# Modulation sums of a two-stream transformer block: sixteen-partition pieces through HBM instead of eight transposes

## The chip, the cores and the metric

The kernel runs on one core of one Trainium2 chip. Its time is the device time of one execution in microseconds (us); lower is better. The engines are TensorE (PE), VectorE (DVE), ScalarE (ACT), GpSimd (POOL) and SyncE (SP), which only issues DMAs. Each engine works through its own instructions in order and waits on semaphores for the others.

## What is computed

Two layers (`DEPTH = 2`) work on two streams of 256 tokens of width 1024: the latents `h` and the context `hc`. Each layer has a feed-forward part, a token mixer and a second feed-forward part. All three are modulated by nine vectors that come from a conditioning vector and a big matrix:

```
mods   = split((silu(c)     @ w_ada[l] + b_ada[l]), 9)      # for h
mods_c = split( silu(c_ctx) @ w_ada[l] + b_ada[l],  9)      # for hc
h = post_norm(h, 0.5 * mods[2] * swiglu(h * (1 + mods[1]) + mods[0], ffn1_up[l], ffn1_down[l]), ln_g[l, 0], ln_b[l, 0])
...                                                          # mixer with mods[3:6], second feed-forward with mods[6:9]
swiglu(u, w_up, w_down) = (silu(u @ w_up[:, :2816]) * (u @ w_up[:, 2816:])) @ w_down
```

The modulation is the subject here: for each layer a product of two rows (c and c_ctx) with a matrix of 1024 x 9216 in float32.

## The kernel before

**Chunks.** All big products run on TensorE in chunks. A chunk of an up loop multiplies 128 columns of a weight (8 tiles of 128x128) with all 512 tokens. Each float32 weight is split into a high and a low part, and each tile takes three matmuls (L909 high times high, L910 and L911 the mixed ones), so a chunk is 24 matmuls of 128x512. The weight of a chunk is loaded by SyncE's queue into one of two raw slots (L713), ScalarE makes the high part `w_hi` (L1342), VectorE the low part `w_lo` (L1932), into one of four split slots. A chunk's split can start when the chunk four places ahead of it has been used; the load of a chunk waits for the split of the chunk two before it. A body of an up loop has four chunks (q = 0 to 3), `UP_BODIES = 11` bodies; a body of a down loop has eight chunks of 6, 6, 5 and 5 tiles, twice, in four bodies.

**Modulation blocks.** The product with `w_ada` is cut into 36 blocks of 512 columns. The first four are made at the start on TensorE. The other 32 are made beside the feed-forward loops: nine in each of three up loops (layer 0 up0 and up1, layer 1 up0), three in layer 0's down0 and two in layer 1's down0 (`ADA_OF`, `ADA_UP`, `ADA_DOWN`). Per block SyncE loads four pieces of 512 KB (L718, j = 0 to 3, two slots), and VectorE multiplies and adds them (`ada_products`, L2307 and L2310): for each of the eight row tiles and both streams one instruction of 128x512, sixteen per block, into two accumulators of 128x512. Piece j + 2 can be loaded once the products of piece j are done. The products of a block fill one body: j = 0 behind the split of q = 0, j = 1 at q = 1, and j = 2 and j = 3 one after the other at q = 2, ahead of the split of q = 3.

What is left is the sum over the 128 partitions. In the next body, behind its first chunk (q = 0), TensorE transposes both accumulators in eight pieces of 128x128 (`ada_columns`, L896) into two PSUM banks; ScalarE then sums each piece along its row with eight activations that accumulate (`ada_totals`, L1524), and VectorE adds the bias at the body's end (`ada_add`, L1971). In a down loop the transposes stand behind q = 6. The first products of the next block wait until the transposes have read the accumulators.

**What sets the order.** The order on each engine is written out by hand in the program, and semaphores tie the engines together: `lo_done` counts VectorE's splits, `ada_mul` its products (16 per block), `ada_turned` the transposed blocks, `ada_ev` the finished ones. SyncE's queue issues in program order: in each step q the weight load of a chunk of the next body, then a modulation load. GpSimd has nearly nothing to do: two clears, a few sums of the layer norm, and 44 products in the last up loop.

## Time and profile before

| | |
|---|---|
| median of 3 runs | 2436.19 us |
| lowest and highest | 2435.21, 2436.35 us |
| span of the profiled execution, first to last instruction | 2432.3 us |
| TensorE busy | 2394.7 us |
| VectorE busy | 1551.8 us |
| ScalarE busy | 1052.7 us |
| GpSimd busy | 61.6 us |
| moved by DMA | 321.83 MB, mean 132 GB/s |

The profile is of one execution. The profiled execution's own device time isn't listed beside its span; the median lies 3.9 us above the span. Times inside it are microseconds from the span's start, durations of one instruction nanoseconds where they stand in a group. A row of a timeline has the start, the duration, the engine, the line of the program, the operation and what it writes and reads; in brackets stands the idle time ahead of it and what ended that. TensorE's matmuls are pipelined, so a matmul's duration (0.39) is longer than the distance to the next start.

### The profile page before, as it was taken

What the parts mean: (1) busy time and instruction counts of PE and PEld (TensorE: products, weight loads), DVE (VectorE), ACT (ScalarE), POOL (GpSimd) and SP (SyncE); (2) the same over time, 40 slices, a digit from 0 to 9 for tenths busy, and PEclk for the clock granted to TensorE, in tenths of its full rate; (3) what the DMA queues carried; (4) which work ended last, traced back from release to release, by engine and by line L of the source; (5) the groups of instructions that cost most, each with busy time, mean ns of one, the idle gap of its engine ahead of it and who ended that gap; (6) DMA issues with size and microseconds to landing.
All of it is one profiled execution on the core that took longest, in us unless ns stands there. A gap on an engine that the chain in (4) does not pass through costs nothing.

```text
span 2432.3 us, 36421 instructions
## 1 busy us (share of the span) xinstructions
PE 2394.7 (98%) x13306; PEld 2064.5 (85%) x13306; DVE 1551.8 (64%) x2584; ACT 1052.7 (43%) x2114; POOL 61.6 (3%) x72
## 2 busy tenths in 40 slices
PE   7999999999999999999999999999999999999998
PEld 4888889887888778898888898888898888999998
DVE  6777467445545445568775367876566556667875
ACT  6533324444333434364343254343245443555544
POOL 0000000000000000020000000000000000001220
PEclk9999999999999999999999999999999999999999
DMA  8666354332222322326663326564434333556654
GB/s 277 182 186 186 97 176 119 86 87 78 61 68 71 91 84 61 113 79 200 185 187 99 96 83 206 178 187 137 143 100 121 105 96 97 163 139 182 191 159 135
DMA packets 519960, 321.83 MB, mean 132 GB/s; under 512 B 14054, under 2 KB 481552, under 8 KB 519824
## 3 DMA queue, kind: packets, MB, share of 16 engines
q1 hardware_dynamic: 518376, 319.63, 45.2%
q8 instruction: 86, 1.41, 0.2%
q10 hardware_dynamic: 1448, 0.38, 0.1%
q14 instruction: 50, 0.41, 0.1%
HBM read 318.92 MB, written 1.05 MB: 132 GB/s over the span
## 4 chain that ended last, share of the span: by engine, by line
PE 88%; DVE 3%; ACT 3%; issue 2%; DMA 2%; SPq 1%; POOL 0%; DVEq 0%; ACTq 0%; POOLq 0%
PE ps L909 26%; PE ps L911 25%; PE ps L910 25%; PE ps L1201 2%; DMA raw<-in_ffn_up 1%; PE ps L992 1%; PE ps L896 1%; PE ps L994 1%; PE ps L993 1%; PE ps L1216 1%; ACT w_hi L1342 1%; PE ps L1177 1%; PE ps L1235 1%; DVE w_lo L1932 1%; SPq L706 1%
## 5 line engine op out<-in xcount | busy, mean ns | idle before, releaser
L1932 DVE TENSOR_TENSOR w_lo<-raw,w_hi 128x1024 fp32r<-128x1024 f32 (+3 forms) x432 | 491.0, 1137 | 584.4 <-ACT w_hi L1342 583.1
L909 PE MATMUL ps<-u_hi,w_hi 128*128 128x512 f32 (+2 forms) x2368 | 860.1, 363 | 1.8 <-DVE scr L2247 1.1
L911 PE MATMUL ps<-u_hi,w_lo 128*128 128x512 f32 (+2 forms) x2368 | 847.8, 358 | 0.0
L910 PE MATMUL ps<-u_lo,w_hi 128*128 128x512 f32 (+2 forms) x2368 | 847.1, 358 | 0.0
L1342 ACT ACTIVATE w_hi<-raw 128x1024 fp32r<-128x1024 f32 (+3 forms) x432 | 426.3, 987 | 911.3 <-PE ps L911 812.9
L911 PEld LDWEIGHTS ps<-u_hi,w_lo 128*128 128x128 f32 x2368 | 446.8, 189 | 65.8
L909 PEld LDWEIGHTS ps<-u_hi,w_hi 128*128 128x128 f32 x2368 | 447.1, 189 | 64.9 <-DVE scr L2247 1.3
L910 PEld LDWEIGHTS ps<-u_lo,w_hi 128*128 128x128 f32 x2368 | 447.2, 189 | 62.9
L909 PE MATMUL ps<-g_hi,w_hi 128*128 128x512 f32 (+1 forms) x704 | 243.8, 346 | 1.3 <-DVE scr L2267 1.3
L911 PE MATMUL ps<-g_hi,w_lo 128*128 128x512 f32 (+1 forms) x704 | 241.2, 343 | 0.0
L910 PE MATMUL ps<-g_lo,w_hi 128*128 128x512 f32 (+1 forms) x704 | 241.2, 343 | 0.0
L909 PEld LDWEIGHTS ps<-g_hi,w_hi 128*128 128x128 f32 x704 | 133.4, 189 | 17.7 <-issue 1.5
L910 PEld LDWEIGHTS ps<-g_lo,w_hi 128*128 128x128 f32 x704 | 133.4, 189 | 16.1 <-issue 0.7
L911 PEld LDWEIGHTS ps<-g_hi,w_lo 128*128 128x128 f32 x704 | 133.4, 189 | 15.5
L2310 DVE SCALAR_TENSOR_TENSOR ada_acc<-ada_in_up,cs,ada_acc 128x512 f32<-128x512 f32 x189 | 141.3, 748 | 0.0
L2310 DVE SCALAR_TENSOR_TENSOR scr<-ada_in_up,cs,scr 128x512 f32<-128x512 f32 x189 | 141.3, 748 | 0.0
L1505 ACT ACTIVATE g_hi<-scr 128x512 f32 (+1 forms) x66 | 41.9, 635 | 169.1 <-DVE scr L2226 169.1
L992 PE MATMUL ps<-u_hi,w_hi 128*128 128x256 f32 (+1 forms) x320 | 93.8, 293 | 8.8 <-DVE u_lo L2056 6.1
L1932 DVE TENSOR_TENSOR w_lo<-h,w_hi 128x1024 fp32r<-128x1024 f32 (+2 forms) x66 | 72.3, 1096 | 36.3 <-ACT w_hi L1342 36.2
L993 PE MATMUL ps<-u_lo,w_hi 128*128 128x256 f32 (+1 forms) x320 | 91.6, 286 | 0.0
L994 PE MATMUL ps<-u_hi,w_lo 128*128 128x256 f32 (+1 forms) x320 | 91.5, 286 | 0.0
L1342 ACT ACTIVATE w_hi<-h 128x1024 fp32r<-128x1024 f32 (+2 forms) x66 | 62.0, 941 | 44.5 <-PE ps L911 44.5
(305 smaller groups left out, 3043.3 us busy)
## 6 DMA issues: line engine op xcount, KB each, us to landing
raw<-in_ffn_up SPq DMA_DIRECT2D x152, 512.0 KB, 3.9
raw<-in_w_in SPq DMA_DIRECT2D x132, 512.0 KB, 3.8
ada_in_up<-in_w_ada SPq DMA_DIRECT2D x108, 512.0 KB, 4.0
raw<-in_ffn_down SPq DMA_DIRECT2D x67, 384.0 KB, 3.4
raw<-in_ffn_down SPq DMA_DIRECT2D x42, 320.0 KB, 3.2
h<-in_ffn_up SPq DMA_DIRECT2D x22, 512.0 KB, 3.8
ada_in_down<-in_w_ada SPq DMA_DIRECT2D x20, 512.0 KB, 4.3
stage<-in_w_ada SPq DMA_DIRECT2D x16, 512.0 KB, 11.4
```

What stands on the lines that cost most here:

```text
L706: sp.dma_start(stage[:, 4 * b + j, :].rearrange("p (k n) -> p k n", k=2), ada_v[0, :, 2 * j:2 * j + 2, b * BLOCK:(b + 1) * BLOCK]).then_in ...
L909: pe.matmul(ps[bank][:, cols_of], wh, a_hi, start=a, stop=False)
L910: pe.matmul(ps[bank][:, cols_of], wh, a_lo, start=False, stop=False)
L911: m = pe.matmul(ps[bank][:, cols_of], wl, a_hi, start=False, stop=b)
L992: pe.matmul(ps[q][:, own], wh, u_hi[:, k, own], start=(k == 0), stop=False)
L993: pe.matmul(ps[q][:, own], wh, u_lo[:, k, own], start=False, stop=False)
L994: m = pe.matmul(ps[q][:, own], wl, u_hi[:, k, own], start=False, stop=(k == KD - 1))
L1201: m = pe.matmul(ps[NUMERATOR[t % 2][n]][:, 0:257], pw[:, n, s, t * P:(t + 1) * P], vaug[:, s, head, :], start=(s == keys[0]), stop=(s == k ...
L1342: act.activation(hi, whole, ACT.Copy).then_inc(hi_done, 1)
L1505: act.activation(g_hi[:, 2 * i + q // 2, t0:TOK], scr[2 + q // 2][:, t0:TOK], ACT.Copy).then_inc(g_hi_done, 1)
L1932: dve.tensor_tensor(lo, whole, hi.bitcast(F32), ALU.subtract).then_inc(lo_done, 1)
L2310: dve.scalar_tensor_tensor(ada_acc[s], w, by, ada_acc[s], ALU.mult, ALU.add).then_inc(ada_mul, 1)
```

## The change

The two accumulators become one tensor `ada_acc` of 128x2x512. When a block's products are done, SyncE's queue stores it to a scratch in HBM (`fold_out`, 512 KB) and loads it back in another shape (`fold`): partition (r, g) holds, for g of the eight column pieces and r of 16 rows, eight rows of 128 numbers. GpSimd adds these eight to one in three steps (four rows at once, two, one; `fold_sums`). The result is one 128x128 tile; TensorE transposes it once, and VectorE sums the 16 values of each piece out of PSUM (`tensor_reduce` in `ada_add`). ScalarE's part falls away.

The order changes with it. The store of a block stands in SyncE's queue in the body after the one with its loads, behind step q = 1, the load-back behind step q = 2 (down loops: q = 2 and q = 3). TensorE's transpose moves from behind q = 0 to behind q = 2 (down loops: from q = 6 to q = 7). VectorE's first products of a block wait until the store of the block before has landed. The SBUF room for `ada_acc` and `fold` comes from below offset 16512, which the program left empty before; `dynamic_dma_scratch_size` of the build is set to 1024 for it.

```diff
+FOLDS = 8
...
-    spot = [16512]
+    spot, low = [16512], [1152]
...
+    ada_acc = below("ada_acc", [P, 2, BLOCK], F32)
+    fold = below("fold", [P, FOLDS, P], F32)
+    fold_out = nc.dram_tensor("fold_out", (P, 2 * BLOCK), F32)
...
-    ada_acc = [scr[4][:, :], ada_acc1[:, :]]
...
 @@ SyncE
+        def store_acc(block):
+
+            sp.wait_ge(ada_mul, 16 * (block - 3))
+            wait(sp, fold_landed, 16 * (block - 4))
+            sp.dma_start(fold_out[:, :], ada_acc[:, :, :].rearrange("p s n -> p (s n)")).then_inc(acc_stored, 16)
+
+        def load_fold(block):
+
+            sp.wait_ge(acc_stored, 16 * (block - 3))
+            wait(sp, ada_turned, block - 4)
+            sp.dma_start(fold[:, :, :], fold_out.ap().rearrange("(q r) (g n) -> (r g) q n", q=FOLDS, n=P)
+                         ).then_inc(fold_landed, 16)
...
 @@ SyncE, up: behind load and ada_load of step q
+                    if block is not None and (not isinstance(i, int) or begin < i <= begin + ADA_UP):
+                        if q == 1:
+                            store_acc(block - begin + i - 1)
+                        elif q == 2:
+                            load_fold(block - begin + i - 1)
...
 @@ SyncE, down
+            pending = ADA_OF[layer, f"up{f}"] + ADA_UP - 1 if ADA_BEGIN.get((layer, f"up{f}")) == 2 else None
...
+                    if i == 0 and pending is not None and q in (1, 2):
+                        (store_acc if q == 1 else load_fold)(pending)
+                    if i and block is not None and i <= ADA_DOWN[layer] and q in (2, 3):
+                        (store_acc if q == 2 else load_fold)(block + i - 1)
...
 @@ TensorE, ada_columns
-            pe.wait_ge(ada_mul, 16 * (block - 3))
-            if isinstance(block, int) and block == 4:
-                pe.wait_ge(ada_ev, 4)
-            else:
-                pe.wait_ge(ada_totalled, block - 4)
-            for s in range(2):
-                for t in range(4):
-                    m = pe.transpose(ps[4 + s][:, t * P:(t + 1) * P], ada_acc[s][:, t * P:(t + 1) * P], ident)
-            m.then_inc(ada_turned, 1)
+            pe.wait_ge(fold_done, block - 3)
+            pe.wait_ge(ada_ev, block)
+            pe.transpose(ps[4][:, 0:P], fold[:, 0, :], ident).then_inc(ada_turned, 1)
...
 @@ TensorE, up and down
-                    if q == 0 and block is not None and (not isinstance(i, int) or begin <= i < begin + ADA_UP):
+                    if q == 2 and block is not None and (not isinstance(i, int) or begin <= i < begin + ADA_UP):
                         ada_columns(block - begin + i)
...
-                    if q == 6 and block is not None and isinstance(i, int) and i < ADA_DOWN[layer]:
+                    if q == 7 and block is not None and isinstance(i, int) and i < ADA_DOWN[layer]:
                         ada_columns(block + i)
...
 @@ ScalarE
-                    if q == 2 and block is not None and (not isinstance(i, int) or begin <= i < begin + ADA_UP):
-                        ada_totals(block - begin + i)
...
 @@ GpSimd
+        def fold_sums(first, count):
+
+            for block in range(first, first + count):
+                pool.wait_ge(fold_landed, 16 * (block - 3))
+                for step, n in enumerate((4, 2)):
+                    pool.tensor_tensor(fold[:, 0:n, :], fold[:, 0:n, :], fold[:, n:2 * n, :], ALU.add
+                                       ).then_inc(fold_half, 1)
+                    pool.wait_ge(fold_half, 2 * (block - 4) + step + 1)
+                pool.tensor_tensor(fold[:, 0, :], fold[:, 0, :], fold[:, 1, :], ALU.add).then_inc(fold_done, 1)
...
 @@ VectorE
         def ada_add(block, layer):
+            dve.wait_ge(ada_turned, block - 3)
+            dve.tensor_reduce(ada_total[:, :, :], ps[4][:, 0:P].rearrange("p (r s t) -> p t s r", s=2, t=4), AXX, ALU.add
+                              ).then_inc(ada_totalled, 1)
...
             if j == 0:
-                wait(dve, ada_turned, block - 4)
+                wait(dve, acc_stored, 16 * (block - 4))
```

On SyncE, in the up loop, from the weight load of step q = 1 to the modulation load of step q = 2 (`raw` are weights, `ada_in_up` modulation loads), before:

```order
L713 DMA raw<-in_ffn_up 128x8x128
L718 ISA [waits ada_mul]
L718 DMA ada_in_up<-in_w_ada 128x2x512
L589 REGISTER_ALU
L713 ISA [waits lo_done]
L713 DMA raw<-in_ffn_up 128x8x128
L589 REGISTER_ALU
L718 ISA [waits ada_mul]
L718 DMA ada_in_up<-in_w_ada 128x2x512
```

and now:

```order
L725 DMA raw<-in_ffn_up 128x8x128
L730 ISA [waits ada_mul]
L730 DMA ada_in_up<-in_w_ada 128x2x512
L601 ISA [waits ada_mul]
L737 DMA fold_out<-ada_acc 128x1024 [waits fold_landed]
L601 REGISTER_ALU
L725 ISA [waits lo_done]
L725 DMA raw<-in_ffn_up 128x8x128
L601 REGISTER_ALU
L730 ISA [waits ada_mul]
L730 DMA ada_in_up<-in_w_ada 128x2x512
L743 DMA fold<-fold_out 128x8x128 [waits ada_turned,acc_stored]
```

The store stands behind the modulation load of q = 1, and the load-back behind the modulation load of q = 2, which itself waits for products.

On TensorE, in the up loop (`con` holds the identity, `scr_78` and `ada_acc_59` are the two accumulators), the end of the chunk q = 0 before:

```order
L910 MATMUL ps<-u_lo,w_hi 128x512
L911 MATMUL ps<-u_hi,w_lo 128x512
L889 REGISTER_ALU
L893 REGISTER_ALU [waits ada_mul]
L896 MATMUL ps<-con,scr_78 128x128 [waits ada_totalled]
L896 MATMUL ps<-con,scr_78 128x128 x3
L896 MATMUL ps<-con,ada_acc_59 128x128 x4
L903 REGISTER_ALU [waits evac_dve]
```

and the end of the chunk q = 2 now:

```order
L939 MATMUL ps<-u_lo,w_hi 128x512
L940 MATMUL ps<-u_hi,w_lo 128x512
L925 REGISTER_ALU [waits fold_done]
L926 MATMUL ps<-con,fold 128x128 [waits ada_ev]
L932 REGISTER_ALU [waits evac_dve]
L938 MATMUL ps<-u_hi,w_hi 128x512 [waits lo_done]
```

Eight transposes have gone from behind q = 0, one stands behind q = 2 and waits for GpSimd.

## Rows read from the trace of the kernel before

**Rows 1.** The page: TensorE's busy share, and the chain that ended last by engine.

```profile
PE 2394.7 (98%) x13306; PEld 2064.5 (85%) x13306; DVE 1551.8 (64%) x2584; ACT 1052.7 (43%) x2114; POOL 61.6 (3%) x72
...
PE 88%; DVE 3%; ACT 3%; issue 2%; DMA 2%; SPq 1%; POOL 0%; DVEq 0%; ACTq 0%; POOLq 0%
```

**Rows 2.** Timeline, TensorE: transposes of two following blocks (start us, duration us, engine, line).

```profile
165.56 0.60 PE L896 MATMUL ps<-con,scr 128*128 128x128 f32 x4
...
188.21 0.60 PE L896 MATMUL ps<-con,scr 128*128 128x128 f32 x4
188.65 0.60 PE L896 MATMUL ps<-con,ada_acc 128*128 128x128 f32 x4
...
189.32 0.39 PE L910 MATMUL ps<-u_lo,w_hi 128*128 128x512 f32 x1
```

**Rows 3.** Timelines of ScalarE, VectorE and SyncE's queue in that body.

```profile
182.97 1.07 ACT L1342 ACTIVATE w_hi<-raw 128x1024 fp32r<-128x1024 f32 x1 [1.54 <-PE ps L911]
...
185.23 1.22 DVE L1932 TENSOR_TENSOR w_lo<-raw,w_hi 128x1024 fp32r<-128x1024 f32 x1
...
190.83 0.48 DVE L2307 TENSOR_SCALAR scr<-ada_in_up,cs 128x512 f32<-128x512 f32 x1
...
192.29 0.75 DVE L2310 SCALAR_TENSOR_TENSOR ada_acc<-ada_in_up,cs,ada_acc 128x512 f32<-128x512 f32 x1
...
186.62 0.37 SPq L713 DMA_DIRECT2D raw<-in_ffn_up  x1
187.19 0.44 SPq L718 DMA_DIRECT2D ada_in_up<-in_w_ada  x1
...
193.21 0.37 SPq L718 DMA_DIRECT2D ada_in_up<-in_w_ada  x1
```

**Rows 4.** DMAs: issues at 187.19 and 193.21, engines at 189, stores, modulation loads' extremes.

```profile
ada_in_up<-in_w_ada SPq DMA_DIRECT2D x1, 512.0 KB, 4.7
...
ada_in_up<-in_w_ada SPq DMA_DIRECT2D x1, 512.0 KB, 3.9
...
189.00:190.00 1.00, 1.00 (x7) 0.84 (x6) 0.31 (x1) 1.00 (x2) 0.00 (x0) 1.00 1.16 369
...
out<-y_out SPq DMA_DIRECT2D x4, 256.0 KB, 2.1
...
DMA to landing us min/median/max: 3.5/4.0/11.4
```

**Rows 5.** Timeline, GpSimd, with VectorE's instructions beside it at 2219.

```profile
1037.48 2.92 POOL L1885 TENSOR_TENSOR scr<-h 128x256 f32<-128x256 f32 x1 [612.73 <-DVE h L2114]
...
1043.73 0.74 POOL L1888 TENSOR_TENSOR scr<-scr,scr 128x256 f32<-128x256 f32 x1
...
2219.17 1.30 DVE L2083 TENSOR_TENSOR h<-h,scr 128x256 f32<-128x256 f32 x2
2219.33 0.85 POOL L1885 TENSOR_TENSOR scr<-scr,h 128x256 f32<-128x256 f32 x1
...
2223.42 1.65 POOL L1885 TENSOR_TENSOR scr<-scr,h 128x256 f32<-128x256 f32 x1 [2.35 <-DVE h L2114]
...
2427.38 1.53 POOL L1905 TENSOR_TENSOR y_out<-y_out,scr 128x512 f32<-128x512 f32 x1
```

**Rows 6.** Timeline of layer 0's down0, first body: VectorE.

```profile
315.83 0.96 DVE L1932 TENSOR_TENSOR w_lo<-raw,w_hi 128x768 fp32r<-128x768 f32 x1 [0.26 <-ACT w_hi L1342]
...
318.69 0.75 DVE L2310 SCALAR_TENSOR_TENSOR ada_acc<-ada_in_down,cs,ada_acc 128x512 f32<-128x512 f32 x1
...
326.22 0.88 DVE L2188 SCALAR_TENSOR_TENSOR h<-ps,gate,h 128x256 f32<-128x256 f32 x2 [2.71 <-PE ps L911]
```

**Rows 7.** A wait of TensorE, and two stretches with their granted clock (last but two).

```profile
41.68 0.36 PE L992 MATMUL ps<-u_hi,w_hi 128*128 128x256 f32 x1 [2.56 <-DVE u_lo L2056]
...
42.00:43.00 1.00, 0.55 (x4) 0.35 (x3) 1.00 (x2) 1.00 (x3) 0.00 (x0) 0.73 1.09 226
...
48.00:50.00 2.00, 2.00 (x14) 2.00 (x13) 0.72 (x2) 2.00 (x5) 0.00 (x0) 0.68 0.67 190
```

More of the change, by code:

```diff
@@ L365, in at, with below @@
         return nc.alloc_sbuf_tensor_at(name, shape, dtype, offset=offset)
+    def below(name, shape, dtype):
+        offset = low[0]
+        low[0] += int(np.prod(shape[1:])) * 4
+        assert low[0] <= 16512, low[0]
+        return at(name, shape, dtype, offset)
+    ada_acc = below("ada_acc", [P, 2, BLOCK], F32)
+    fold = below("fold", [P, FOLDS, P], F32)
+    fold_out = nc.dram_tensor("fold_out", (P, 2 * BLOCK), F32)
     h = at("h", [P, KD, TOK], F32)
@@ L555, in build @@
     ada_mul, ada_turned, ada_totalled = (sem(n) for n in ("ada_mul", "ada_turned", "ada_totalled"))
+    acc_stored, fold_landed, fold_half, fold_done = (
+        sem(n) for n in ("acc_stored", "fold_landed", "fold_half", "fold_done"))
     ln_pivot, ln_pivot_out, ln_cent, ln_sq, ln_added, ln_rest = (
@@ L1085, in down @@
                 if block is not None:
-                    pe.wait_ge(ada_totalled, block + ADA_DOWN[layer] - 4)
+                    pe.wait_ge(ada_ev, block + ADA_DOWN[layer])
                 part(0, i, segs[1][1], bank=LAST_DOWN[0], after_k=4, then=lambda: statistics(n, 0))
@@ L1460, in up @@
             t0 = t0_of(layer) if f else 0
-            block = ADA_OF.get((layer, f"up{f}"))
-            begin = ADA_BEGIN.get((layer, f"up{f}"))
             n = 3 * layer + 2 * f
@@ L1515, in up @@
             body(UP_BODIES - 1)
-        def ada_totals(block):
-            act.wait_ge(ada_turned, block - 3)
-            wait(act, ada_ev, block)
-            for s in range(2):
-                for t in range(4):
-                    own = ps[4 + s][:, t * P:(t + 1) * P]
-                    m = act.activation(own, own, ACT.Copy, accum_out=ada_total[:, t, s:s + 1])
-            m.then_inc(ada_totalled, 1)
         def down(layer, f):
             base = BASES[layer, f"down{f}"][0]
-            block = ADA_OF.get((layer, f"down{f}"))
             n = 3 * layer + 2 * f + 1
@@ L1534, in body @@
                     ahead(base, q, i, 8, down_kn(q))
-                    if q == 6 and block is not None and isinstance(i, int) and i < ADA_DOWN[layer]:
-                        ada_totals(block + i)
             body(0)
@@ L1888, in late_sums @@
                     pool.tensor_tensor(scr[2][:, seg], scr[2][:, seg], scr[1][:, seg], ALU.add).then_inc(ln_added, 1)
+        def fold_sums(first, count):
[6 more added lines that the diff above has]
+                pool.tensor_tensor(fold[:, 0, :], fold[:, 0, :], fold[:, 1, :], ALU.add).then_inc(fold_done, 1)
         for layer in range(DEPTH):
+            fold_sums(ADA_OF[layer, "up0"], ADA_UP)
+            fold_sums(ADA_OF[layer, "down0"], ADA_DOWN[layer])
             pool.wait_ge(chunk_used, BASES[layer, "down0"][0] + 4 * KD)
@@ L1894, in _ @@
             late_sums(3 * layer + 2)
+            if layer == 0:
+                fold_sums(ADA_OF[0, "up1"], ADA_UP)
         pool.wait_ge(up_spread, 2)
@@ L2306, in ada_products @@
                     if j == 0 and e == 0:
[L2307 removed]
+                        dve.tensor_scalar(ada_acc[:, s, :], w, by, None, ALU.mult).then_inc(ada_mul, 1)
                     else:
                         dve.wait_ge(ada_mul, n + 2 * e + s - 1)
[L2310 removed]
+                        dve.scalar_tensor_tensor(ada_acc[:, s, :], w, by, ada_acc[:, s, :], ALU.mult, ALU.add
                                                  ).then_inc(ada_mul, 1)
@@ L2846 @@
     from concourse.bass_utils import run_bass_kernel_spmd as _run
-    nc = _bacc.Bacc("TRN2", target_bir_lowering=False, num_devices=1)
+    nc = _bacc.Bacc("TRN2", target_bir_lowering=False, num_devices=1, dynamic_dma_scratch_size=1024)
     arrays, args = {}, []
```

2 lines of the change are left out of this document (removed).

## The prediction

> **What bounds the kernel now.** I first read the page's busy shares and its chain of waits [rows 1]: TensorE is busy 98% of the span and makes up 88% of the chain that ended last. So time is won only by taking work off TensorE, and any wait put into TensorE's order costs its full length. The timeline of TensorE comes second [rows 2]: in the up loops the eight transposes of one block follow the next in 22.65 us (165.56 to 188.21). The matmul that starts at 189.32 is one matmul step p behind the end of the transposes, so the transposes take x = 1.11 - p, and 96 matmuls take 22.65 - x: p = 0.227 us, x = 0.88 us. A chunk of 24 matmuls is 5.44 us, a body of four 21.77 us. Third, the timelines of VectorE and SyncE's queue over the same body [rows 3]: they show when a block's products end and when the queue issues. I compare the new path of a block with that clockwork.
>
> **What is removed.** Eight transposes become one. The eight took 0.88 us; for one I take 0.15 us, between 0.11 (an eighth of it) and 0.3 (a new weight and a semaphore wait may not overlap). All 32 blocks, all on the path: 32 x 0.73 = 23 us saved, bounds 19 to 25. ScalarE loses sixteen short instructions a block; no saving, it isn't in the chain. VectorE gains a 128x128 reduction, below the 0.75 us of its 128x512 instruction [rows 3], at the body's end, long after the transpose and with nobody waiting for it there: 0.
>
> **What is added, in the up loops.** TensorE now waits after the third chunk of body i for GpSimd's last addition. It reaches that point 2 x 5.44 us after 188.21, with the transposes gone from there: at 199.1. The path of the same block, in the times of this body:
> 1. Its last product ends at 185.23; the SyncE queue first waits for the split that follows, issues the weight load at 186.62 and the modulation load at 187.19 for 0.44 us [rows 3]. The store is issued at 187.7.
> 2. The modulation load landed 4.7 us after its issue, 191.9, and the DMA engines ran at 369 GB/s with a share above 1 [rows 4]: one queue, already full. The 0.5 MB store behind it needs 1.4 us more: 193.3. Lower bound: a 256 KB store landed in 2.1 us alone; 0.7 more for the second half is 2.8, at 190.5.
> 3. VectorE's first product of the next block overwrites the sums, so it now waits for the store: 193.3 instead of 190.83. The four products take 2.21 us (190.83 to 193.04): 195.6.
> 4. SyncE's load of the third pair of modulation rows waits for just those products (before: products end 193.04, issue 193.21 [rows 3]); the load-back stands behind it in the same queue: issued 196.2. This is a knot: the products wait for the store, the queue for the products, and the load-back for the queue.
> 5. A modulation load lands in 3.9 us with a free queue; the load-back behind it 1.4 later: 201.1. Lower bound 3.5 us from its own issue [rows 4].
> 6. GpSimd's three additions. A 128x256 addition took 0.74 us, a 128x512 one 1.53 with some waiting [rows 5]. I take 1.4 + 0.74 + 0.37 and 0.2 for two semaphores: 2.7. Alone they end at 203.8, 4.7 us after TensorE's arrival.
>
> GpSimd is not alone. At 2219.17 two VectorE additions with two SBUF inputs took 1.30 us together while a GpSimd addition took 0.85, and at 2223.42 a GpSimd addition needed 1.65 instead of 0.74 [rows 5]: the two engines take turns. The split of the fourth-next chunk and eight products of VectorE lie exactly here. With one VectorE instruction between each two of GpSimd's, the first wait is 6.3 us. The Trainium skill (GPSIMD Engine Reference, Key points) says the same in general: GpSimd shares its SBUF interfaces with VectorE and contends with VectorE instructions that have two SBUF inputs. The trace agrees.
>
> A wait shifts what follows. After a wait w TensorE arrives w later, plus 0.15 for the transpose. The store shifts less, since the split ahead of it would have been ready at 184.1 (ScalarE's row at 182.97 [rows 3]) and stood behind products until 185.23: w - 1.1. So later waits are shorter by 1.1 + 0.15: the load-back lands 0.8 us after TensorE's arrival, the first addition runs to 2.3, VectorE's split to 3.4, the second to 4.1, a product to 4.8, the third to 5.2. Later waits: 5.2 us (3.5 if GpSimd were undisturbed). Each of three up phases has nine blocks. The last has no next products to wait for and no modulation load in the queue: its load-back is issued near 191.8, ends near 198.5, no wait. Sum: 3 x (6.3 + 7 x 5.2) = 128 us. Undisturbed: 3 x (4.7 + 7 x 3.5) = 88.
>
> **In the down loops** (five blocks) the transpose moves behind the eighth chunk. Before, that chunk ended just before VectorE's row at 326.22, now 0.9 earlier: 325.2. The products end at 319.4 [rows 6]; store issued 319.5, landed 322.3, load-back issued 322.4, landed 326.3, additions with one or two turns of VectorE until 330.0: 4.8 us of wait, 24 us for five.
>
> **The clock.** TensorE's granted clock was 1.00 nearly everywhere, but after a wait of 2.56 us among sparse matmuls it fell at about 42.5 us and rose again before 50 [rows 7]: 0.73 means half speed in part of that microsecond, and the low stretch adds to 6.8 us, which costs 3.4 us if TensorE works throughout. The new waits of about 5 us are longer than that one. So I expect a fall (2.4 to 1.2 GHz) in each of 24 + 5 = 29 waits; part of a low stretch lies inside the wait, so I take 2.3 us each, bounds 0 and 3.4: 67 us. The Trainium skill (TensorE: Matmul & The Clock Gate, Why this matters for your kernels) warns of idle gaps between matmul bursts; in this trace only that one stretch and the end of the program show it.
>
> **Sum** against the profiled execution: 2432.3 - 23 + 128 + 24 + 67 = 2628 us of span. The median is 3.9 us above the span, which I leave as it is: 2632.
>
> **Rivals.**
> - The clock holds at 2.4 GHz through the waits: 2632 - 67 = 2565. For it: only one fall in mid-program. Against: no wait of this length inside the loops before.
> - GpSimd is not disturbed: waits of 3.5, down 3.8; clock falls seldom: 2436 - 23 + 88 + 19 = 2520. Against: [rows 5].
> - GpSimd is kept out through VectorE's whole train of eight products (5.3 us). One addition did take 2.92 us beside back-to-back VectorE instructions [rows 5]. Waits near 9.6 us, 24 x 9.7 = 233, down 28, clock 67: 2741. Against: at 2219 GpSimd came in between two VectorE instructions.
> - Transfers land at their lower bounds: store at 190.5, so the products aren't held, load-back issued 193.7, landed 197.2, additions until 199.7. First wait 0.6, then 0.3 on average since each wait gives the next some slack: 8 us; down 3 x 5 = 15; no clock falls: 2436 - 23 + 23 = 2436, no change.
> - The other side: the path is finished before TensorE arrives and the 23 us are a clean gain: 2413. It decides at 12.7 us between the split's end (186.4) and 199.1; my path needs 17.4, the lower bounds 13.3. It needs the store and the weight loads to overlap in the queue and the additions to run near VectorE's speed. The slack is otherwise there: DMA engines are idle half of the time, and GpSimd is idle.
>
> **How the numbers follow.** Forecast 2632 (0.45; alone 2590 to 2690), clock holds 0.18, GpSimd undisturbed 0.15, GpSimd kept out 0.05, no change 0.07, clean gain 0.10. A measurement of this kernel can tell 0.2%, about 5 us. Faster 0.12 (the last and part of the one before), same 0.05, slower 0.83. Range 2500 to 2745: it leaves out the last two and takes in the bounds of contention and clock.
>
> **What would show it.** TensorE rows of the transpose with idle time of 5 to 6 us, released by GpSimd, 24 times in the up loops, and none for the last block of a phase; 5 in the down loops. VectorE's first product of a block held by the store for 2 us or so. The load-back issued about 9.8 us after the split's end and landing 4.9 later. GpSimd's 128x512 addition near 1.4 and the second and third stretched. The granted clock at 0.5 for some microseconds behind each wait. If the transpose starts without idle time, steps 2 to 5 are wrong; if the waits are there and the clock stays at 1.00, only its term is.

## The result and the profile after

The changed kernel takes 2668.05 us (median of 4 runs, 2666.29 to 2668.40) where the kernel before takes 2435.7 us beside it: ratio 1.0957, 95% interval 1.0943 to 1.0971 (a ratio is always to the kernel before, measured beside it). It is slower, by 232 us. The forecast was 2632 us, range 2500 to 2745. The profiled execution has a span of 2665.9 us, and TensorE's mean granted clock fell from 0.998 to 0.958.

The page of the changed kernel: span, busy time, the granted clock in 40 slices, the chain that ended last by engine, the transpose's group of instructions (count, busy us, mean ns, idle us before it), and the two new transfers (count, KB, median us from issue to landing).

```profile
span 2665.9 us, 35660 instructions
...
PE 2451.0 (92%) x13082; PEld 2093.6 (79%) x13082; DVE 1611.8 (60%) x2616; ACT 977.3 (37%) x1602; POOL 171.2 (6%) x168
...
PEclk9888899999999999998888999888989999999999
...
PE 66%; DMA 14%; DVE 6%; POOL 4%; issue 4%; ACT 4%; SPq 2%; DVEq 0%; ACTq 0%; POOLq 0%
...
L926 PE MATMUL ps<-con,fold 128*128 128x128 f32 x32 | 14.5, 452 | 178.8 <-POOL fold L1910 178.8
...
fold_out<-ada_acc SPq DMA_DIRECT2D x32, 512.0 KB, 6.0
fold<-fold_out SPq DMA_DIRECT2D x32, 512.0 KB, 5.4
```

Against [rows 1]: TensorE has 224 matmuls fewer (7 transposes in each of 32 blocks) and yet 56 us more busy time, since it runs at half clock in part of it; its share of the chain fell from 88 to 66%, and transfers rose from 2 to 14%. The digit 8 in the clock's row stands where the three up loops are, and once in layer 1's down0. One wait explains most: TensorE stood 178.8 us before its one transpose a block, released by GpSimd.

Its timeline, transposes only (start, duration, engine and line, in brackets the idle time before it and who ended it): block 4, two blocks in the loop, the last block of the first phase, the first of the second, the last of the second, and a down block.

```profile
101.16 0.48 PE L926 MATMUL ps<-con,fold 128*128 128x128 f32 x1 [15.32 <-POOL fold L1910]
...
222.09 0.47 PE L926 MATMUL ps<-con,fold 128*128 128x128 f32 x1 [5.76 <-POOL fold L1910]
252.63 0.47 PE L926 MATMUL ps<-con,fold 128*128 128x128 f32 x1 [5.76 <-POOL fold L1910]
...
339.60 0.33 PE L926 MATMUL ps<-con,fold 128*128 128x128 f32 x1 [0.68 <-POOL fold L1910]
...
437.90 0.48 PE L926 MATMUL ps<-con,fold 128*128 128x128 f32 x1 [4.26 <-POOL fold L1910]
...
1222.60 0.48 PE L926 MATMUL ps<-con,fold 128*128 128x128 f32 x1 [8.80 <-POOL fold L1910]
...
1461.77 0.29 PE L926 MATMUL ps<-con,fold 128*128 128x128 f32 x1
```

Where [rows 2] had 22.65 us from block to block, there are now 30.54 (30.2 to 30.8 in this phase without its first and last body). The first waits of the three up phases are 15.32, 8.80 and 8.66 us, the 21 later ones 5.59 to 6.33 (nearly all 5.67 or 5.76), the last block of a phase waits 0.68, 0 and 0, and the five down blocks 4.26 to 6.49.

The path of the block that is transposed at 252.63, in the timelines of VectorE, SyncE's queue and GpSimd (they answer [rows 3] and [rows 5]); the last two rows are GpSimd in the phase's last block, where VectorE has no products:

```profile
231.78 1.23 DVE L1958 TENSOR_TENSOR w_lo<-raw,w_hi 128x1024 fp32r<-128x1024 f32 x1 [5.95 <-ACT w_hi L1371]
...
240.41 0.88 DVE L2336 TENSOR_SCALAR ada_acc<-ada_in_up,cs 128x512 f32<-128x512 f32 x2 [1.88 <-DMA fold_out<-ada_acc]
...
249.31 7.05 DVE L2339 SCALAR_TENSOR_TENSOR ada_acc<-ada_in_up,cs,ada_acc 128x512 f32<-128x512 f32 x8
```

```profile
234.37 0.38 SPq L737 DMA_DIRECT2D fold_out<-ada_acc  x1
...
242.78 0.37 SPq L730 DMA_DIRECT2D ada_in_up<-in_w_ada  x1
243.25 0.42 SPq L743 DMA_DIRECT2D fold<-fold_out  x1
```

```profile
248.81 2.83 POOL L1907 TENSOR_TENSOR fold<-fold 128x512 f32<-128x512 f32 x2 [26.86 <-DMA fold<-fold_out]
251.72 0.78 POOL L1910 TENSOR_TENSOR fold<-fold 128x128 f32<-128x128 f32 x1
...
336.51 2.43 POOL L1907 TENSOR_TENSOR fold<-fold 128x512 f32<-128x512 f32 x2 [22.66 <-DMA fold<-fold_out]
339.01 0.45 POOL L1910 TENSOR_TENSOR fold<-fold 128x128 f32<-128x128 f32 x1
```

The split ends at 233.01, the store is issued at 234.37 and lands at 240.41 (6.0 us), the four products end at 242.62, the load-back is issued at 243.25, just behind the modulation load of 242.78, and it lands at 248.81 (5.6 us), and GpSimd's three additions take 3.7 us. That is 19.5 us of one thing after another, and TensorE is there at 252.63 - 5.76 = 246.87, 13.9 after the split's end.

The granted clock around that wait, TensorE alone (us, busy us and matmuls, clock, share and GB/s of the DMA engines):

```profile
250.00:251.00 1.00, 0.00 (x0) 1.00 1.01 342
251.00:252.00 1.00, 0.00 (x0) 0.87 0.98 296
252.00:253.00 1.00, 0.36 (x2) 0.50 0.80 225
...
258.00:259.00 1.00, 1.00 (x5) 0.71 0.00 0
259.00:260.00 1.00, 1.00 (x6) 1.00 0.00 0
```

The clock falls while TensorE still waits, from 1.00 to 0.50 (2.4 to 1.2 GHz), and is back at 258.6, 6 us after work has begun again. Over the program the trace has 31 such low stretches, 228 us together, where before there were two with 13 us (that of [rows 7] and the program's end).

### The profile page after: what moved, and what is told of

Same layout as the page of the kernel before. It is cut to its first block, busy times and chain, and to the rows that moved or that the text cites. A ratio compares the mean times of both kernels' runs of the same rounds, so it can differ in the third digit from the quotient of the medians.

```text
span 2665.9 us, 35660 instructions
## 1 busy us (share of the span) xinstructions
PE 2451.0 (92%) x13082; PEld 2093.6 (79%) x13082; DVE 1611.8 (60%) x2616; ACT 977.3 (37%) x1602; POOL 171.2 (6%) x168
## 4 chain that ended last, share of the span: by engine, by line
PE 66%; DMA 14%; DVE 6%; POOL 4%; issue 4%; ACT 4%; SPq 2%; DVEq 0%; ACTq 0%; POOLq 0%
PE ps L938 19%; PE ps L939 18%; PE ps L940 18%; DMA fold_out<-ada_acc 6%; DMA fold<-fold_out 6%; POOL fold L1907 3%; PE ps L1230 2%; ACT w_hi L1371 2%; DVE ada_acc L2339 2%; DVE w_lo L1958 2%; PE ps L1021 1%; PE ps L1023 1%; PE ps L1022 1%; SPq L730 1%; POOL fold L1910 1%
## 5 line engine op out<-in xcount | busy, mean ns | idle before, releaser
L938 PE MATMUL ps<-u_hi,w_hi 128*128 128x512 f32 (+2 forms) x2368 | 888.2, 375 | 2.0 <-DVE scr L2276 1.1
L939 PE MATMUL ps<-u_lo,w_hi 128*128 128x512 f32 (+2 forms) x2368 | 870.3, 368 | 0.0
L940 PE MATMUL ps<-u_hi,w_lo 128*128 128x512 f32 (+2 forms) x2368 | 869.3, 367 | 0.0
L938 PEld LDWEIGHTS ps<-u_hi,w_hi 128*128 128x128 f32 x2368 | 462.7, 195 | 71.1 <-issue 1.5
L940 PEld LDWEIGHTS ps<-u_hi,w_lo 128*128 128x128 f32 x2368 | 460.9, 195 | 72.1
L939 PEld LDWEIGHTS ps<-u_lo,w_hi 128*128 128x128 f32 x2368 | 463.3, 196 | 67.9
L2339 DVE SCALAR_TENSOR_TENSOR ada_acc<-ada_in_up,cs,ada_acc 128x512 f32<-128x512 f32 x378 | 297.6, 849 | 0.2
L926 PE MATMUL ps<-con,fold 128*128 128x128 f32 x32 | 14.5, 452 | 178.8 <-POOL fold L1910 178.8
L1907 POOL TENSOR_TENSOR fold<-fold 128x512 f32<-128x512 f32 x64 | 85.5, 1336 | 1196.2 <-DMA fold<-fold_out 1193.7
L926 PEld LDWEIGHTS ps<-con,fold 128*128 128x128 f32 x32 | 5.7, 177 | 191.7 <-issue 124.8
```

The lines of the kernel that those rows point to most:

```text
L938: pe.matmul(ps[bank][:, cols_of], wh, a_hi, start=a, stop=False)
L939: pe.matmul(ps[bank][:, cols_of], wh, a_lo, start=False, stop=False)
L940: m = pe.matmul(ps[bank][:, cols_of], wl, a_hi, start=False, stop=b)
L1907: pool.tensor_tensor(fold[:, 0:n, :], fold[:, 0:n, :], fold[:, n:2 * n, :], ALU.add).then_inc(fold_half, 1)
L2339: dve.scalar_tensor_tensor(ada_acc[:, s, :], w, by, ada_acc[:, s, :], ALU.mult, ALU.add).then_inc(ada_mul, 1)
```

## The experiments

All edits are to the changed kernel. Spans are of the profiled executions; one account of all kernels stands at the end of this part. "The loop" means the up loops' blocks but the first and the last of each phase; a phase is one up loop.

**The queue's order in the up loops, both transfers.** The store and the load-back go ahead of the modulation load of the same chunk:

```diff
                     load(raw_place(base, q, i, 4), ...)
+                    if block is not None and (not isinstance(i, int) or begin < i <= begin + ADA_UP):
+                        if q == 1:
+                            store_acc(block - begin + i - 1)
+                        if q == 2:
+                            load_fold(block - begin + i - 1)
...
-                    if block is not None and (not isinstance(i, int) or begin < i <= begin + ADA_UP):
-                        if q == 1:
-                            store_acc(block - begin + i - 1)
-                        elif q == 2:
-                            load_fold(block - begin + i - 1)
```

> In the up loops the store and the load-back stand ahead of the modulation load of their step in SyncE's queue, instead of behind it; nothing else. Theory (knot): the store lands 1.4 us earlier, the load-back no longer waits for VectorE's next products and for the load ahead of it, 4 us more; TensorE's wait in the up loops falls from 5.8 us to about 0.5, the clock stays at 1.00 there, the down loops are unchanged: about 2470 us (2455 to 2500). Rival (the extra traffic and GpSimd's share of the SBUF slow everything, wherever the commands stand): stays near 2668. Rival (GpSimd's additions are what takes the time): the wait falls by 1.4 us only, about 2630.

Measured: 2526.24 us, ratio 1.0382 (1.0364 to 1.0399). Waits in the loop of 1.4 to 2.9 us (most 1.5 to 2.3) in place of 5.76; block 4 still 12.95, the five down blocks 23.7 in all (24.3 before). The queue and GpSimd in the middle of the first phase:

```profile
206.78 0.41 SPq L737 DMA_DIRECT2D fold_out<-ada_acc  x1
...
211.68 0.37 SPq L725 DMA_DIRECT2D raw<-in_ffn_up  x1
212.15 0.53 SPq L743 DMA_DIRECT2D fold<-fold_out  x1
```

```profile
217.79 2.62 POOL L1907 TENSOR_TENSOR fold<-fold 128x512 f32<-128x512 f32 x2 [20.24 <-DMA fold<-fold_out]
```

The store landed 5.0 us after its issue (6.0 before). The direction was right, but 56 us of what I expected didn't come: the load-back has the weight load of 211.68 ahead of it and takes 5.6 us all the same.

**The load-back alone.** Only the second half of that edit, the store stays behind the modulation load:

> The changed kernel with one transfer moved: SyncE issues the load-back ahead of the third modulation load and not behind it; the store stays where it is. The step of the prediction that I called a knot says that the load-back waits in the queue for VectorE's four products. If that knot alone makes the wait, the load-back is issued when the store has landed (6.0 us after its issue) and no later than the split, about 2.5 to 3 us sooner than in the changed kernel, and doesn't stand behind a 512 KB load in the transfer either; waits of 5.7 fall to about 2.5, with less clock lost: 24 x (3.2 + 1.5) = 113 us less, 2555. The kernel with both moved took 2526, so the store's place would be worth 30. If the store's place is what counts, this one stays above 2620.

Measured: 2538.20 us, ratio 1.0421 (1.0405 to 1.0437). So the load-back's place in the queue carries 130 of the 232 us, and moving the store too brings 12 more. It is mostly the knot that the prediction named (products wait for the store, the queue for the products, the load-back for the queue); the rest is a quicker landing, since the edit also takes the modulation load away from ahead of the load-back. The queue, GpSimd and a transpose:

```profile
238.16 0.38 SPq L737 DMA_DIRECT2D fold_out<-ada_acc  x1
242.49 0.37 SPq L725 DMA_DIRECT2D raw<-in_ffn_up  x1
244.20 0.37 SPq L743 DMA_DIRECT2D fold<-fold_out  x1
```

```profile
248.87 2.42 POOL L1908 TENSOR_TENSOR fold<-fold 128x512 f32<-128x512 f32 x2 [20.50 <-DMA fold<-fold_out]
```

```profile
252.28 0.32 PE L927 MATMUL ps<-con,fold 128*128 128x128 f32 x1 [1.61 <-POOL fold L1911]
```

The load-back now goes out as soon as the store has landed (244.20) and not 2.8 us after it, and lands in 4.7 us, not 5.6, with the last load issued 1.7 us ahead of it and not 0.5. Together 3.7 us a block, 2.8 of them the knot, and most waits in the loop fell from 5.76 to between 1.5 and 2.5.

**The transpose one chunk later.** In the up loops only:

```diff
-                    if q == 2 and block is not None and (not isinstance(i, int) or begin <= i < begin + ADA_UP):
+                    if q == 3 and block is not None and (not isinstance(i, int) or begin <= i < begin + ADA_UP):
```

> TensorE's transpose of a block stands behind the fourth chunk (q = 3) of the up body instead of the third; nothing else. Theory: TensorE works one chunk (5.44 us) more before it asks, so waits of 5.8 us become about 0.5 and the clock stays: about 2475 us (2460 to 2510). Rival (traffic and shared SBUF): near 2668. Rival (the wait moves with it, since the next chunk's split waits for what TensorE does): near 2650.

Measured: 2514.14 us, ratio 1.0330 (1.0313 to 1.0347). A chunk is 5.44 us and the wait was 5.76, but waits of 0 to 2.6 us stay. With TensorE no longer held, VectorE comes to its limit; its timeline in one body:

```profile
210.80 0.88 DVE L2336 TENSOR_SCALAR ada_acc<-ada_in_up,cs 128x512 f32<-128x512 f32 x2 [3.59 <-DMA fold_out<-ada_acc]
...
219.05 7.11 DVE L2339 SCALAR_TENSOR_TENSOR ada_acc<-ada_in_up,cs,ada_acc 128x512 f32<-128x512 f32 x8
```

It loses 3.6 us to the store, and its last eight products take 1.7 us longer beside GpSimd (7.11 against 5.38 in the kernel before), in a body in which it is busy for 80% of the time (19.9 of 25 us). My 2475 left that out.

**The clock alone, twelve fillers.** Before the wait, TensorE does matmuls that nobody reads, so that it isn't idle:

```diff
+            for _ in range(12):
+                pe.matmul(ps[5][:, :], mean_w, con[:, 0:512], start=True, stop=True)
             pe.wait_ge(fold_done, block - 3)
```

> TensorE does 12 matmuls of 128x512 in float32 into an unused bank ahead of each wait for GpSimd (about 0.43 us each, 5.2 us together); they compute nothing that is used. Theory (clock): the waits of 5.8 us are filled, the granted clock stays at 1.00 in the up loops, each of 24 blocks loses the 3.0 us of the low clock (72 us), the five down blocks some 10 us, while the three blocks that didn't wait pay 5.2 us each: about 2600 us. Rival (the low clock costs nothing, since TensorE would wait for the chain anyway): 2668 or 15 us more.

Measured: 2745.6 us, ratio 1.1279. The size was wrong: a plain float32 filler stands in the trace as two matmuls and took 0.855 us, so twelve of them took 10.3 us, more than the wait. The run tells little of the clock's price, only that with no idle time the clock stays up (0.996).

**Six fillers** instead of twelve, 5.1 us:

> As the run with twelve filler matmuls, but with six: the run before showed that one takes 0.855 us, so six are 5.1 us, just under the waits of 5.8. They compute nothing that is used. Theory (the low clock is a cost of its own, on top of the wait): the clock stays at 1.00, the wait that is left is about 0.6 us, a body of the up loops takes 21.8 + 0.2 + 5.8 = 27.7 instead of 30.7 us; 24 x 3.0 less, five down blocks 2 less each, three last blocks 5.1 more each: 2668 - 72 - 10 + 15 = 2600 us. Rival (with the clock up the chain alone sets the pace and TensorE just waits longer): 2668 or above.

Measured: 2618.89 us, ratio 1.0756 (1.0738 to 1.0774). Every digit of the page's clock row is a 9. Two transposes:

```profile
215.75 0.33 PE L928 MATMUL ps<-con,fold 128*128 128x128 f32 x1 [0.61 <-POOL fold L1912]
243.70 0.32 PE L928 MATMUL ps<-con,fold 128*128 128x128 f32 x1 [0.61 <-POOL fold L1912]
```

TensorE is kept from its real work for 5.13 + 0.61 = 5.74 us a block, as in the changed kernel (5.76), and the period is 27.95 us, not 30.6. So 2.6 us a block are the clock's and not the wait's. It is 49 us faster in all, although blocks that had no wait pay for fillers too. I had expected 2600: I had put 3.0 us on each of 24 blocks, and the first waits of the phases are longer than six fillers (10.95, 4.21 and 4.34 us of them stay). The Trainium skill (TensorE: Matmul & The Clock Gate, Why this matters for your kernels) warns of idle gaps between matmul bursts; the two traces agree that it is the idling, since the same delay filled with matmuls leaves the clock at 1.00.

**Without GpSimd's first two additions** (the sums are then incomplete), to see what they and VectorE's turns beside them are worth:

```diff
-                for step, n in enumerate((4, 2)):
-                    pool.tensor_tensor(fold[:, 0:n, :], fold[:, 0:n, :], fold[:, n:2 * n, :], ALU.add
-                                       ).then_inc(fold_half, 1)
-                    pool.wait_ge(fold_half, 2 * (block - 4) + step + 1)
```

> GpSimd's first two additions (128x512 and 128x256) are left out, so seven of the eight rows are partly not summed; the third stays. It prices GpSimd's part of the chain. Theory: each wait is shorter by what the two additions took, 2.8 us: from 5.8 to about 3.0, 24 x 2.8 + 5 x 2.5 = 80 us; with the clock still falling each time 2590 us, with the clock held some 60 less, 2530. Rival (GpSimd was the bound, with VectorE in its way): waits vanish, about 2460. Rival (transfers alone): under 20 us, 2650.

Measured: 2549.82 us, ratio 1.0470. Waits in the loop are 2.96 us, 2.8 less, which is what the two additions took (2.83). The time fell by 118 us, more than the 80 us that the waits lost (178.8 to 98.9): the low stretches went from 228 to 108 us as well, mostly 3.4 us long where they were 6.8. That lies between my two cases (2590 with a full fall of the clock, 2530 with none).

**Both of the first edits together**, the queue's order and the later transpose:

> Both cures in the up loops: store and load-back ahead of the modulation loads, and the transpose behind the fourth chunk. Down loops unchanged. Theory: the path of a block then has 5 us of room, the up waits vanish but for the very first block (5 to 7 us) and the clock stays; what remains is the down loops' 24 us of wait and about 12 of clock: 2436 - 20 + 7 + 24 + 12 = 2459 us. Rival (traffic and GpSimd's share cost time of their own): above 2500.

Measured: 2469.10 us, ratio 1.0145 (1.0128 to 1.0162). What is left is 23 us in the five down blocks (4.3 to 4.9 each), 7.4 at block 4, some 2.5 at the starts of the later phases, and their clock.

**And the down loops** (e6 in the texts below). The transpose behind the second chunk of the next body, where nothing waits; VectorE's reduction and bias move with it (not shown in these lines):

```diff
-                    if q == 7 and block is not None and isinstance(i, int) and i < ADA_DOWN[layer]:
-                        ada_columns(block + i)
+                    if q == 1 and block is not None and 1 <= i <= ADA_DOWN[layer]:
+                        ada_columns(block + i - 1)
...
```

> As the one before, and in the down loops the transpose of a block stands behind the second chunk of the next body, VectorE's reduction and bias behind its third split. Theory: no wait is left but the first block's; TensorE keeps the 20 us of the transposes that went: 2436 - 20 + 7 = 2423 us (2412 to 2432), faster than the kernel before. Rival (the transposes' 0.88 us were hidden or the extra DMA traffic delays weight loads): 2436 or slower.

Measured: 2437.13 us (10 runs), ratio 1.0010 (1.0001 to 1.0020): the 232 us are gone, and nothing is won. TensorE still waits 14.7 us in five places, and its clock falls four times ahead of the program's end, once where the kernel before has its own fall [rows 7].

**The order in the peeled body** (e9: e6 with this edit). A peeled body is one that is written out ahead of the loop. Block 4 waited 7.4 us there because in the second body of the first phase VectorE has the next block's first products ahead of the split, and so the split, the queue's weight load and the load-back behind it stood still for the store:

```diff
-                    first = q == 3 or q == 0 and not inner and i == 1
+                    first = q == 3 or q == 0 and not inner and i == 1 and begin == 2
```

> The kernel of e6 with one further edit: in the first up phase, VectorE's first products of block 5 stand behind the split of their chunk as in every other body, not ahead of it. In e6 the split stood behind two products that waited 2.75 us for the store, the queue's weight load and the load-back behind it were issued only at 88.6, and TensorE waited 7.4 us at block 4, followed by a low stretch of 10.2 us. My theory (the wait at block 4 is made by the order in VectorE's peeled body) expects that wait to shrink to 3 us or less, the low stretch with it, and 2437 - 4.5 - 3 = 2430 us. Rival (the load-back is late there because the first phase's transfers are slow whatever the order): the wait stays near 7 and the time at 2437.

Measured: 2434.39 us (11 runs), ratio 0.9999 (0.9990 to 1.0008). The wait at block 4 fell from 7.39 to 2.80 us, so 4.6 us of it are the order's, but only 2.7 us of the time came of it; one block later stands a wait of 1.8 that was not there. Some of its transposes:

```profile
93.40 0.48 PE L926 MATMUL ps<-con,fold 128*128 128x128 f32 x1 [2.80 <-POOL fold L1912]
118.76 0.33 PE L926 MATMUL ps<-con,fold 128*128 128x128 f32 x1 [1.82 <-POOL fold L1912]
142.56 0.27 PE L926 MATMUL ps<-con,fold 128*128 128x128 f32 x1
...
208.30 0.27 PE L926 MATMUL ps<-con,fold 128*128 128x128 f32 x1
231.82 0.32 PE L926 MATMUL ps<-con,fold 128*128 128x128 f32 x1 [1.46 <-POOL fold L1912]
255.91 0.27 PE L926 MATMUL ps<-con,fold 128*128 128x128 f32 x1
```

Undisturbed bodies take 21.9 us (142.56 to 208.30 in three), about 0.74 less than the 22.65 of [rows 2]: this is the saving that the change is capable of, and it is there. Then one wait of 1.46 us costs 1.6 us in its own body and 2.2 in the next (255.91 - 231.82 = 24.09), of which a low stretch of 3.4 us behind the wait explains 1.7: together 3.8 us, the saving of five blocks. The windows behind that wait (us, busy us and matmuls, clock, share and GB/s of the DMA engines):

```profile
233.00:234.00 1.00, 1.00 (x4) 0.53 0.00 0
234.00:237.00 3.00, 3.00 (x9) 0.59 0.55 175
237.00:238.00 1.00, 1.00 (x7) 1.00 0.06 8
```

Where does that wait come from? GpSimd and VectorE in that block and in the one before it, which had no wait:

```profile
203.09 2.48 POOL L1909 TENSOR_TENSOR fold<-fold 128x512 f32<-128x512 f32 x2 [18.89 <-DMA fold<-fold_out]
...
225.75 5.07 POOL L1909 TENSOR_TENSOR fold<-fold 128x512 f32<-128x512 f32 x2 [19.31 <-DMA fold<-fold_out]
```

```profile
201.86 4.26 DVE L2341 SCALAR_TENSOR_TENSOR ada_acc<-ada_in_up,cs,ada_acc 128x512 f32<-128x512 f32 x4
...
224.07 2.73 DVE L2341 SCALAR_TENSOR_TENSOR ada_acc<-ada_in_up,cs,ada_acc 128x512 f32<-128x512 f32 x4
```

The load-back landed 4.6 us before TensorE asked, in time for additions of the usual 3.0 to 3.9 us. But here the first addition (128x512) took 3.94 us instead of 1.33, and all three 5.9, while VectorE's four products kept their full pace; in the block before, GpSimd kept its pace and VectorE's products were stretched. Four of this kernel's six waits (1.82, 1.46, 2.89 and 2.67 us of 12.0) stand at blocks whose additions took 5.4 to 5.9 us. With additions of 3.5 us they would come to about 1.2 us (an estimate from the landings, 3.0 to 4.6 us before TensorE asks). What decides which engine is held up no run took apart.

**Without HBM** (e8). Eight transfers of 64 KB take the sums from 128 partitions straight to the pieces; the load-back is gone, VectorE's next products wait for the eight landings, and the queue waits for the transpose of the block before ahead of the first issue. The transpose stands where the change has it, the down loops as above:

```diff
...
-            sp.dma_start(fold_out[:, :], ada_acc[:, :, :].rearrange("p s n -> p (s n)")).then_inc(acc_stored, 16)
+            for q in range(FOLDS):
+                sp.dma_start(fold[:, q, :], ada_acc[16 * q:16 * q + 16, :, :].rearrange("r s (t n) -> r (s t) n", n=P)
+                             ).then_inc(fold_landed, 16)
...
```

> No HBM scratch: eight DMAs of 64 KB copy the sums straight from SBUF to SBUF in the pieces' shape, at the store's place behind the modulation load; the transpose stays behind the third chunk, the down loops' is moved as in the run before. Theory (two passes through one full queue and the knot with VectorE's products are the chain): with one pass the pieces land about 6 us after the first issue, at 194 of the body whose TensorE arrives at 199.1, GpSimd is done by 197.5, no wait: 2436 - 20 + 6 = 2422 us. Rival (a copy inside SBUF or eight issues take longer than 9 us): waits of some us stay, 2450 to 2530.

Measured: 2491.55 us, ratio 1.0232. Waits of 0.95 to 2.94 us in nearly all up blocks (the next text says 1.2 to 2.5 in most), 5.94 at block 4. Was that only the position? The same with the transpose behind the fourth chunk:

> The kernel of e9, but the sums don't go through HBM: eight 64 KB transfers take them from the 128 partitions to the 16-partition pieces directly, and stand behind the modulation load of the second chunk. One landing instead of two. With the transpose behind the third chunk (e8) TensorE still waited 1.2 to 2.5 us in most blocks; behind the fourth it has 5.4 us more, so my theory (what is left in e8 is only the position) expects no waits in the up loops and 2415 to 2425 us: 2413 of the clean gain and up to 10 for the starts of the phases. Rival (the eight issues of 0.6 us each hold up SyncE's queue, so weight loads come late and VectorE and TensorE with them): periods above 21.9 us and 2440 or more.

Measured: 2475.23 us, ratio 1.0166 (1.0153 to 1.0180): the rival won. The queue and VectorE in one body:

```profile
255.13 5.07 SPq L738 DMA_DIRECT2D fold<-ada_acc  x8
260.46 0.39 SPq L725 DMA_DIRECT2D raw<-in_ffn_up  x1
```

```profile
262.02 2.46 DVE L2337 TENSOR_SCALAR ada_acc<-ada_in_up,cs 128x512 f32<-128x512 f32 x2 [3.85 <-DMA fold<-ada_acc]
```

Eight issues hold SyncE for 5.1 us, VectorE stands 3.85 us for the last of them, and then its first two products take 2.46 us and not 0.88, since GpSimd's additions start at the same moment. VectorE's period is 24.8 us, and TensorE can't be faster. One landing was saved and paid for in issues and in VectorE's time; the shares of the two were not taken apart.

**One account for all of them.** From the span I take 2408.9, which is the span before (2432.3) less the 23.4 us saved (32 x 0.73, the predicted figure); what is left is split into TensorE's waits before the transposes and a rest. Beside it stands half the sum of the low stretches (at half clock, half of a stretch is lost), less the 6.4 us that the kernel before has by the same count; and last the same without the parts that lie inside the waits, where TensorE had nothing to do.

| kernel | span - 2408.9 | waits | rest | half of low stretches | outside the waits |
|---|---|---|---|---|---|
| changed | 257.0 | 178.8 | 78 | 108 | 81 |
| without two additions | 140.7 | 98.9 | 42 | 48 | 40 |
| load-back ahead | 127.8 | 93.8 | 34 | 40 | 30 |
| both ahead | 111.3 | 84.7 | 27 | 32 | 23 |
| transpose later | 103.2 | 67.3 | 36 | 32 | 24 |
| both ahead, later | 58.9 | 36.6 | 22 | 25 | 19 |
| and the down loops | 27.7 | 14.7 | 13 | 12 | 10 |
| and block 4 | 25.9 | 12.0 | 14 | 12 | 12 |
| direct | 85.5 | 57.7 | 28 | 24 | 22 |
| direct, later | 64.3 | 35.6 | 29 | 16 | 15 |

Waits and the last column account for every kernel that goes through HBM to within 4 us, but for the one with only the transpose moved, where 12 us are left over. In the changed kernel 27 of the 108 lie inside the waits. In the two direct kernels 6 and 13 us are left over. VectorE's pace is the likely reason in all three (24 to 25 us a body instead of 21.9); no run took it apart. The two filler kernels close as well: with 5.13 us of fillers in each of 32 blocks, 164 + 33 of waits + 9 of clock = 206 against 208, and with 10.26 us, 328 + 6 + 4 = 338 against 336.

## Why the prediction held

The sign, the mechanism and the time (2632 against 2668, 1.4% low) were right, the time with some luck in it, since errors of single steps cancel in part. By its steps:

- **Saved.** 0.73 us a block were put down; the undisturbed bodies of the last kernels show 0.74, so the one transpose costs about 0.14 us (21.91 less the 21.77 of 96 matmuls), where 0.15 was put down. VectorE's reduction (0.28 us) cost nothing.
- **Store.** Issued 1.3 us after the split's end by the prediction, 1.36 measured; landing 5.6 against 6.0. The products behind it 2.21 and 2.21, and the knot: load-back issued 0.6 after the products, measured 0.63. The run with only the load-back moved shows the knot as a cause and not only as a sequence: it is 2.8 of the 3.7 us a block that this edit gains.
- **Load-back.** 4.9 against 5.6: of a block's steps this one was too small by the most. It was built from a landing with a free queue plus 1.4 for the load before it; the changed kernel as a whole also loads slower, 4.4 us for a modulation load by the median, where it was 4.0 [rows 4].
- **GpSimd.** 2.7 alone and 4.4 between VectorE's instructions were put down; 2.95 and 3.7 measured. It gets its turns, and VectorE pays: its eight products took 7.05 us, and 5.38 where GpSimd isn't adding. The rival of a GpSimd kept out through VectorE's train is out for this kernel (no block's additions took over 4.1 us), that of an undisturbed one too; but in the kernels with the transfers ahead, blocks with additions of 5.4 to 6.1 us do turn up.
- **Waits.** Later ones 5.2 against 5.76; the shift rule (later waits start with slack from the one before) was right, TensorE arrives 13.9 us after the split as it gave (12.7 + 1.1). The load-back was too small by 0.7 us and the store by 0.4, the additions too large by 0.7. Next to no wait in a phase's last block, as said (0.68, 0 and 0). Down 4.8 against a mean of 4.86.
- **First waits.** 6.3 was said, 8.80 and 8.66 came, and 15.32 at block 4. This step failed: it took the clockwork of a body in the middle for the first one. TensorE was to come 12.7 us after the split's end; it came 10.1 and 10.3 us after it in the second and third phase (at 1213.80, the split's end at 1203.73), and 6.6 at block 4. The trace of before has it: at the first transposes of the second phase the split ends 1.1 us after they start, where in [rows 2] and [rows 3] it ends 1.8 us before (rows below). At block 4 the path is longer too, 21.9 us: the store takes 6.9 to land, and the products stand ahead of the split there, so the queue's weight load and the load-back wait for the store as well; the edit of that order alone took 4.6 us from the wait in its kernel. Cost: 3 x 6.3 = 19 against 33.

```profile
1113.79 1.23 DVE L1932 TENSOR_TENSOR w_lo<-raw,w_hi 128x1024 fp32r<-128x1024 f32 x1
...
1113.94 0.66 PE L896 MATMUL ps<-con,scr 128*128 128x128 f32 x4
```

- **Clock.** 29 falls and 2.3 us for each were put down, 67 in all. The 29 falls came; the account gives 78 as the rest, the fillers show 2.6 a block, and a body itself 30.54 - 21.91 - 5.76 = 2.9. The reasoning holds (part of a low stretch lies inside the wait): of the 6.8 us from 251.7 to 258.6, 0.9 lie inside it, and half of the other 5.9 is 2.95.

In sum: waits 179 in place of 152 (14 of the 27 at the first blocks, 12 in the loop at 0.6 each), clock 78 in place of 67, saving 23 as said. The 3.9 us between median and span were wrong as well, on the other side: the changed kernel's profiled execution took 2667.9 us against a span of 2665.9, 2.0 us more, and executions of the kernel before lie about 1.8 above their spans. The rival "clock holds" (2565) fell with the fillers and with the windows of the clock; "the other side", a clean gain at 2413, needed the path within 12.7 us, and it took 19.5. Its slack does exist at the body's end: with the transpose there (in the down loops in the next body), the transfers ahead in the queue and block 4's order mended, the waits vanish in 26 of 32 blocks.

But that kernel isn't faster than the one before. The last 26 us are six short waits, four of them in the first four blocks of a phase, and five falls of the clock, and they cancel the 23 us saved. No kernel here beats the one before. Most of these waits, the 1.46 us at 231.82 too, go with a first addition of GpSimd that took 3.4 to 3.9 us instead of 1.3 to 2.0; why it does so in some blocks is open. So is whether another engine's queue for the store and the load-back, which would go past the knot without a new order, gains anything: no run tried it.

## What to carry to other kernels

Moving work off the bounding engine pays only what that work costs there (0.74 us a block here), while a path of store, load-back and additions that ends late costs its whole lateness and, where the clock falls, half of the low stretch that lies behind the wait. Before such a change, lay the new path against the moment at which the bounding engine arrives, with every queue it passes: what stood worst here was one queue entry, a load-back behind a load that waited for the very products that waited for the store. Put the consumer as late as the data allow, put the transfers ahead of loads that aren't urgent, and look at the first body by itself. Leave room for the slowest case of a step that shares something with another engine: the additions usually took 3.0 to 3.9 us, but 3.0 to 4.6 us of room weren't enough here, since some took 5.9.

## What the runs showed of the hardware

- A 512 KB store to HBM took 6.0 us from issue to landing behind two 512 KB loads issued just before it, 5.0 behind one; the load-back 5.6 behind a load, 4.7 where the last load had been issued 1.7 us earlier. I had 5.6 and 4.9. The Trainium skill (DMA: Bandwidth & Descriptors, Anatomy of one DMA — SWDGE (gpsimd) path) says of transfers issued on GpSimd's path that the fixed part is mostly the wait until the last byte is confirmed as landed, longest when HBM is written. The transfers here are issued by SyncE, and no run separates that part.
- Eight transfers of 64 KB issued from one queue take 5.1 us to issue, as long as one transfer of 512 KB needs from issue to landing (5.0).
- GpSimd's additions and VectorE's instructions stretch each other: the 128x128 addition took 0.45 us alone and 0.78 beside products. It isn't only VectorE instructions with two SBUF tensors as inputs: the two first products of a block (TENSOR_SCALAR, one tensor) took 0.88 us alone and 2.46 when GpSimd's largest additions fell on them. Which engine loses differs from block to block: four products 4.26 us and the 128x512 addition 1.33, or 2.73 us and 3.94.
- The clock's cost depends on the wait: waits of about 5.76 us went with low stretches of 6.8 us, waits of 2.96 with 3.4 in most cases, and one of 1.46 with one of 3.4 too, while most waits of 1.5 to 2.3 had none.
